# Memory attention phases: the value projection with memory tokens stationary, and the first query weights ahead of the constants

## The reference, cut to what matters

```python
def memory_attention(q_mem, mem_n, w_mem_kv):      # mem_n: (b, 256, 1024), w_mem_kv: (1024, 2048)
    q = q_mem.reshape(b, t, 4, 256) * (256 ** -0.5)
    kv = (mem_n @ w_mem_kv).reshape(b, m, 2, 4, 256)
    k, v = kv[:, :, 0], kv[:, :, 1]
    s = einsum('bthd,bmhd->bhtm', q, k)
    return einsum('bhtm,bmhd->bthd', softmax(s), v)
# in both layers: h = rmsnorm(x, pre_g[i]); mem_n = rmsnorm(mem, mem_g[i]); proj = h @ w_in -> ..., q_mem, gate z
# x = x + rmsnorm(concat(mixer * gate, memory * gate) @ w_out[i], post_g[i])
```

## Time and profile before

| | |
|---|---|
| median of 3 executions | 2368.26 us |
| the profiled execution: its time | 2366.96 us |
| the profiled execution: its span, first to last instruction | 2365.2 us |
| PE busy | 2187.3 us (92%) |
| PE weight loads (beside the matmuls) | 1876.9 us (79%) |
| DVE busy | 1080.8 us (46%) |
| POOL busy | 913.2 us (39%) |
| ACT busy | 729.9 us (31%) |
| granted clock, mean | 0.969 |
| layer 0's V units | about 79 to 134 us of the span |
| layer 1's V units | about 1175 to 1238 us |

### The profile page before, as it was taken

How to read it: one execution, slowest core, us unless ns; L and a number is a source line. 1 busy time by engine, 2 the same in 40 slices (tenths; PEclk the granted TensorE clock), 3 DMA queues, 4 the chain that set the end, 5 groups by cost and what they waited for, 6 DMA issues and landing times. The chain is left out here.

```text
span 2365.2 us, 32257 instructions
## 1 busy us (share of the span) xinstructions
PE 2187.3 (92%) x13362; PEld 1876.9 (79%) x13362; DVE 1080.8 (46%) x1686; ACT 729.9 (31%) x1662; POOL 913.2 (39%) x624
## 2 busy tenths in 40 slices
PE   6989999899999999985989999799999999999995
PEld 5778887688788888874768887688888888888884
DVE  3203333686787778774650223123432334333235
ACT  3113122343343335342322221032423233242332
POOL 3533332232333332331643332444544444454443
PEclk9999999899999999997999999899999999999998
DMA  5221112334222322222631110232222212212111
GB/s 173 78 63 48 54 54 75 107 80 131 81 90 63 116 72 90 63 71 81 195 118 51 54 48 33 61 124 62 62 70 61 59 56 62 70 58 66 54 45 54
DMA packets 228622, 180.59 MB, mean 76 GB/s; under 512 B 23323, under 2 KB 204859, under 8 KB 228475
## 3 DMA queue, kind: packets, MB, share of 16 engines
q1 hardware_dynamic: 228475, 178.52, 24.4%
HBM read 168.71 MB, written 12.21 MB: 76 GB/s over the span
## 5 line engine op out<-in xcount | busy, mean ns | idle before, releaser
L214 PE MATMUL bank<-Hh,Wh 128*128 128x256 f32 (+1 forms) x2192 | 756.4, 345 | 31.5 <-POOL Wl L191 13.0
L188 POOL TENSOR_SCALAR Wh<-Wraw 128x1024 fp32r<-128x1024 f32 x217 | 243.3, 1121 | 1327.3 <-issue 764.4
L214 PE MATMUL bank<-Hl,Wh 128*128 128x256 f32 (+1 forms) x2192 | 742.1, 339 | 0.0
L214 PE MATMUL bank<-Hh,Wl 128*128 128x256 f32 (+1 forms) x2192 | 740.6, 338 | 0.0
L191 POOL TENSOR_TENSOR Wl<-Wraw,Wh 128x1024 fp32r<-128x1024 f32 x217 | 539.8, 2487 | 18.1
L214 PEld LDWEIGHTS bank<-Hh,Wh 128*128 128x128 f32 x2192 | 420.5, 192 | 81.5 <-issue 24.1
L214 PEld LDWEIGHTS bank<-Hh,Wl 128*128 128x128 f32 x2192 | 419.7, 191 | 44.1
L214 PEld LDWEIGHTS bank<-Hl,Wh 128*128 128x128 f32 x2192 | 420.7, 192 | 40.9 <-issue 1.7
L264 PE MATMUL bank<-Wh,Mh 128*128 128x512 f32 x552 | 224.7, 407 | 47.2 <-issue 20.6
L288 DVE TENSOR_TENSOR acc<-bank,acc 128x512 f32<-128x512 f32 x240 | 165.7, 691 | 220.9 <-PE bank L264 220.1
L264 PE MATMUL bank<-Wh,Ml 128*128 128x512 f32 x552 | 221.5, 401 | 0.0
(11 more groups left out here) (203 smaller groups left out, 2689.7 us busy)
## 6 DMA issues: line engine op xcount, KB each, us to landing
Wraw<-in_na_w_in_dram SPq DMA_DIRECT2D x80, 512.0 KB, 3.7
Wraw<-in_ssd_w_in_dram SPq DMA_DIRECT2D x57, 512.0 KB, 4.0
Wraw<-in_w_out_dram SPq DMA_DIRECT2D x48, 512.0 KB, 3.6
R<-acs_dram SPq DMA_DIRECT2D x16, 1536.0 KB, 6.3
Wraw<-in_w_mem_kv_dram SPq DMA_DIRECT2D x32, 512.0 KB, 3.9
R<-gs_dram SPq DMA_DIRECT2D x32, 128.0 KB, 3.5
macc_dram<-acc SPq DMA_DIRECT2D x1, 3072.0 KB, 10.2
R<-macc_dram SPq DMA_DIRECT2D x6, 512.0 KB, 5.4
```

The source lines that it names most:

```text
L188: pool.tensor_scalar(Wh[:, s, :], Wraw[:, s, :], 1.0, 1.0, ALU.mult, ALU.mult).then_inc(pool_c, 1)
L214: mm = pe.matmul(DB[h.k % 2][:, 0:t1 - t0], w[:, k, :], x[:, k, t0:t1], start=(k == 0 and i == 0), stop=(k == KC - 1 and i == 2))
```

## The change

V units now have the orientation of `pe_out`. Unit 8+u holds 256 rows (two blocks of the contraction) by 512 columns of V; the four token tiles of `Mem_h`/`Mem_l` are stationary, and the 512 weight columns move. Four units make one half of the features, which accumulates in four banks at once: `A[4]`, `A[5]`, `DB[0]`, `DB[1]`. ACT evicts each bank straight into `vtok`. The transposes, `vF` and DVE's copies are gone. The second half takes the banks in the order 2, 3, 0, 1. PE waits for all eight evictions (`v_taken`) ahead of the first query unit. In layer 0 SP now loads both q0 units ahead of the constants.

```diff
-            order = ["kv"] * 16 + ["q0"] * 2
+            order = ["k"] * 8 + ["v"] * 8 + ["q0"] * 2
...
+            V_BANK = [A[4], A[5], DB[0], DB[1]]
+            V_ORDER = [(0, 1, 2, 3), (2, 3, 0, 1)]
...
-                    load_f(sp, wkv, slice(u * P, (u + 1) * P))
+                    if u < 8:
+                        load_f(sp, wkv, slice(u * P, (u + 1) * P))
+                    else:
+                        half, j = (u - 8) // 4, u % 4
+                        load_unit(sp, wkv[j * 256:(j + 1) * 256, D + half * 512:D + (half + 1) * 512]
+                                  .rearrange("(k p) c -> p k c", p=P), 2)
...
+                load_head(0, q_col)
                 if pre is not None:
                     sp.wait_ge(x_norm.turned, 2 * NT)
                     pre.sync(sp, None)
-                load_head(0, q_col)
...
-                def take_v(u):
-                    if u >= 2:
-                        act.wait_ge(v_turned, u - 1)
-                    act_take(act, [lambda b: act.activation(vF[u % 2], b[:, :], ACT.Copy)])
+                def take_v(half):
+
+                    for _ in range(4):
+                        U["act"].next()
+                    for i, t in enumerate(V_ORDER[half]):
+                        if i < 3:
+                            act.wait_ge(v_done, 3 * half + i + 1)
+                        else:
+                            act.wait_ge(unit_done, U["act"].value + 2)
+                        act.activation(vtok[:, t, half * 512:(half + 1) * 512], V_BANK[t][:, :], ACT.Copy)\
+                            .then_inc(v_taken, 1)
...
+                    x_norm.act_turned(act, 0)
                     take_v(0)
-                    for u in range(1, 8):
-                        take_v(u)
-                        if u >= 2:
-                            x_norm.act_turned(act, u - 2)
+                    for i in range(1, NT - 1):
+                        x_norm.act_turned(act, i)
+                    take_v(1)
+                    x_norm.act_turned(act, NT - 1)
...
-                def take_v(u):
-                    dve.wait_ge(v_turned, u + 1)
-                    dve.tensor_copy(vtok[:, :, u * P:(u + 1) * P],
-                                    A[4 + u % 2][:, :].rearrange("p (t f) -> p t f", t=4)).then_inc(v_taken, 1)
...
+                pe.wait_ge(out_added, OF["pe"].value + 2)
+                pe.wait_ge(dense_free, HF["pe"].value + 1)
                 for u in range(8):
-                    pe_dense(pe, kv, H=(Mem_h, Mem_l))
-
-                    pe.wait_ge(dense_free, HF["pe"].value + 2)
-                    if u >= 2:
-                        pe.wait_ge(v_taken, u - 1)
+                    half, j = u // 4, u % 4
+                    w, s = U["pe"], U["pe"].k % 2
+                    pe.wait_ge(w_ready, w.value + 3)
+                    wh = Wh[:, s, :].rearrange("p (k c) -> p k c", k=2)
+                    wl = Wl[:, s, :].rearrange("p (k c) -> p k c", k=2)
+                    for i, t in enumerate(V_ORDER[half]):
+                        tok = slice(t * P, (t + 1) * P)
+                        if u == 0 and i == 3:
+                            pe.wait_ge(dense_free, HF["pe"].value + 2)
+                        if half and j == 0:
+                            pe.wait_ge(v_taken, V_ORDER[0].index(t) + 1)
+                        for k in range(2):
+                            for p, (x, y) in enumerate(((Mem_h, wh), (Mem_l, wh), (Mem_h, wl))):
+                                mm = pe.matmul(V_BANK[t][:, :], x[:, 2 * j + k, tok], y[:, k, :],
+                                               start=(j == 0 and k == 0 and p == 0), stop=(j == 3 and k == 1 and p == 2))
+                        if i == 3:
+                            mm.then_inc(unit_done, 1)
+                        elif j == 3:
+                            mm.then_inc(v_done, 1)
+                    w.next()
                     if u >= TURN_X - 8 >= 0:
                         x_norm.pe(pe, u - TURN_X + 8)
-                    for t in range(4):
-                        mm = pe.transpose(A[4 + u % 2][:, t * P:(t + 1) * P], vF[u % 2][:, t * P:(t + 1) * P],
-                                          ident[:, :])
-                    mm.then_inc(v_turned, 1)
+                pe.wait_ge(v_taken, 8)
                 x_norm.pe_end(pe)
```

More of the change, by code:

```diff
@@ L479, in memory_phase @@
                 post_gain = r(D)
-                vF = [post_gain[:, 0:512], post_gain[:, 512:1024]]
                 macc, res = mem[:, 0:2, :], mem[:, 2:4, :]
                 post = [r(NT) for _ in range(3)]
-            else:
-                vF = [mem[:, 2, 0:512], mem[:, 3, 0:512]]
             with ExitStack() as kv_only:
@@ L494, in memory_phase @@
             gain_landed = sem(n + "gain_landed")
-            v_turned, v_taken, scored, max_ready, prob_ready, prob_normed = (
-                sem(n + x) for x in ("v_turned", "v_taken", "scored", "max_ready", "prob_ready", "prob_normed"))
+            v_done, v_taken, scored, max_ready, prob_ready, prob_normed = (
+                sem(n + x) for x in ("v_done", "v_taken", "scored", "max_ready", "prob_ready", "prob_normed"))
             p_turned, pT_ready, mixed, gate_ready, hi_ready = (
@@ L534, in halves @@
             def halves(units):
-                return sum(1 if u == "kv" else 0 if u[:3] == "out" else 2 for u in units)
+                return sum(1 if u == "k" else 0 if u == "v" or u[:3] == "out" else 2 for u in units)
+            V_BANK = [A[4], A[5], DB[0], DB[1]]
+            V_ORDER = [(0, 1, 2, 3), (2, 3, 0, 1)]
             def evicted(name):
@@ L648, in scalar @@
                         x_norm.act_turned(act, u - TURN_X)
-                    for u in range(8):
-                        take_v(u)
+                    for half in range(2):
+                        take_v(half)
                 else:
@@ L877, in tensor @@
                     pe.wait_ge(pT_ready, h * 3 + 3)
-                    pe.wait_ge(v_taken, 8)
                     v = vtok[:, :, h * 256:(h + 1) * 256]
```

## The result

| | before | after |
|---|---|---|
| median | 2368.39 us (4 executions, 2364.78 to 2369.49) | **2345.75 us** (4 executions, 2343.75 to 2350.09) |
| ratio, 95% interval | 1 | **0.9909** [0.9892, 0.9927] |
| the profiled execution: time, span | 2366.96, 2365.2 us | 2344.77, 2343.1 us |

Forecast 2345.1 us, in a range of 2339 to 2351: 22.6 us were gained by the medians, 21.8 were forecast. The steps held less exactly than the sum: the changed parts gave 2.2 us less than I wrote, and chance gave it back in the profiled execution. (The profiled execution of experiment 11 took 4732 us for a cause that its trace does not show; it is left out of all numbers.)

The account below looks back on a forecast made before the run. PE, busy 92% of the span, was taken as the bound. Gains of 10.1 us in layer 0 and 11.7 in layer 1 sum to 21.8, so 2366.96 becomes 2345.1 us, range 2339 to 2351.

Parts of the forecast that it names:

- The seams: PE's idle and transposes between old V units, 1.27 us each; the seven waits inside layer 0's phase should have no successor.
- the end: When PE could start the next matmul after a unit's last: 0.23 us behind that last matmul's start.
- The price of a V matmul: V units: 0.2266 us a matmul as in the output projection, so 24 matmuls cost 5.44 us.
- my upper bound of 5.54: V unit's time at the old shape's matmul price: 5.54 us, 1.5 us more over 15 units.
- The queue: Layer 0 loads: z0's weights 28.33 us behind unit 17's load; the wait moves from q0 to z0, lasting 7.4 us.
- The slow start at z0: Layer 0 behind the wait at z0: clock 0.50 costs 1.98 us as before; could be 2 less or up to 2 more.
- Layer 1's tail: From the last V unit's end to q0 in layer 1: 4.0 us instead of 5.1, gain 1.1.
- The sum: Whole program: 10.1 us from layer 0 plus 11.7 from layer 1, 21.8 us gained.
- (a): Rival at layer 0's z0: the wait vanishes because the constants pass quicker, 2335.7 us; chance 8%.
- (b): Rival in the V phase: POOL's splits or slow loads bound it, a unit taking 5.8 us, 2350.5 us; chance 5%.
- (c): Rival in the V phase: bank turns leave PE idle and the clock drops to 0.50, 2432 us; chance 4%.
- (d): Rival in layer 0: something other than the constants held q0's weights, q0 at 136.85, 2351 us; chance 5%.

Follow-up runs that it names:

- experiment 11: The changed kernel run again unedited, beside the kernel before: ratio 0.9918, four executions of 2345.2 to 2352.1 us.
- experiment 8: Changed kernel, but layer 1's V matmuls take stationary tiles from Mh and Ml instead of Mem_h and Mem_l: 2345.84 us, one execution.
- experiment 10: Changed kernel plus whole-row ssd_d, two later PE waits, and layer 1's memory tokens aligned to 64 bytes at byte 129216: 2341.53 us, ratio 0.9881.
- experiment 12: Changed kernel plus whole-row ssd_d, two later PE waits, and both layers' memory tokens at a multiple of 128 bytes: 2332.11 us, ratio 0.9841.
- experiment 3: Changed kernel with ssd_d loaded as whole rows of 32 numbers, DVE picking the halves out: 2338.24 us, ratio 0.9869.
- experiment 5: Changed kernel with one of ssd_d's two single-number transfers kept, the other half taken from a whole row: 2337.68 us, ratio 0.9868.
- experiment 1: Changed kernel with SP's old order, the constants again between the loads of units 15 and 16: 2353.53 us, ratio 0.9935.
- experiment 4: Changed kernel with the two ssd_d transfers, still 4-byte runs, issued from ACT's queue early in the V phase: 2352.72 us, ratio 0.9929.

## Why the prediction was right, and where it was not

- **The seams.** All seven of layer 0's idle stretches are gone, and no wait for `v_taken` came at unit 12. q0 starts 0.85 behind the end and at 123.52, forecast 123.6. But this agreement is two errors: V began 1.19 us earlier by chance, and seven units took 1.12 us more than forecast.
- **The price of a V matmul** is the step that failed: "24 matmuls cost 5.44 us", taken from the earlier trace rows as having "the same moving tile and shape". It measured 5.60 and 5.62, above my upper bound of 5.54 too, and in layer 1 above the 5.6 that I had named as a sign of being wrong. The rows priced the shape rightly and left out where the stationary operand lies: `Mh` at a multiple of 128 bytes, `Mem_h` 64 or 96 above one (experiments 8, 10, 12). It cost 0.8 us at z0 (five units, since that wait hangs on unit 13's end) and 1.3 in layer 1 (7 x 0.18), less 0.3 for five tiles at 0.88 us, forecast 0.94.
- **The queue.** The step "28.33 us from the load ahead to the first weights behind" held to 0.1 us in three orders. The wait moved from q0 to z0 and lasts 6.76 us, forecast 7.4: unit 17's load left at 115.44 in place of 115.83 (1.19 early with all the rest, 0.8 late by its five units), and z0's weights came 0.5 earlier with it, while q0 began as forecast.
- **The slow start at z0** was taken as 1.98 us, as before. From z0's start to the split behind its first unit it took 158.49 - 147.21 = 11.28 us, where before, without a wait, it took 8.69 (159.82 to the split below), so 2.6 us: 0.6 more, within its bound.

Timeline of POOL in the kernel before, the split behind z0's first unit:

```profile
168.51 1.05 POOL L188 TENSOR_SCALAR Wh<-Wraw 128x1024 fp32r<-128x1024 f32 x1 [4.82 <-issue]
```

- **Layer 1's tail.** ACT begins the last high part at 1217.63, 0.69 behind the end (0.80 forecast), DVE at 1218.76, q0 starts 4.0 behind the end, as forecast.
- **The sum.** 8.8 + 10.75 = 19.6 us, where the text has 21.8. The profiled execution came to 2344.77 only with 1.19 us at its start and 2.3 at its end that are no part of the change. Right to 0.03% was luck; right to 0.1% would have been earned. How much luck, experiment 11 says: four more executions of the same kernel have a median of 2351.1.
- **The rivals.** (a) fell: the passage is constant, even when other loads surround it, and experiments 3 and 5 name what it is made of. (b) fell by its mechanism, though a V unit did get longer: POOL waits 2.07 us for PE at each unit. (c) fell: clock 1.00 from 79 to 122. The rule on depth-cycling of the Trainium skill (TensorE: Matmul & The Clock Gate, "A second HAM failure mode: psum-queue depth-cycling") was not put to the test: it tells of small idle gaps, and with four open banks PE had none, 43.00 us busy of 43. (d) fell by experiment 1 against the change: 4.7 us at the same place, and a wait of 13.44 us at q0.

## What to carry to other kernels

When a matmul's price is read from another place of the program, compare where both operands lie in a partition as well as their shapes, and put the operands of long matmuls at a multiple of 128 bytes; here that was 3% of a matmul. A transfer made of single numbers stopped SP's loads here, whether SP or ACT issued it: load whole rows and let an idle engine pick the numbers out. A reordering that fills a wait is worth what the wait is then, so price it together with what shortens the work in front of it.

## What the runs showed of the hardware that I had not expected

- Two transfers of 1024 numbers of 4 bytes hold the DMA for 16 to 18 us at a share of 0.05 and 0 GB/s, and loads of 512 KB on another engine's queue stand still too (experiment 4).
- The distance between matmuls of 512 columns depends on where the tokens' tensor begins: 0.2267 to 0.2277 us at a multiple of 128 bytes, 0.2333 at 64 above one, 0.2343 at 96, as stationary operand (experiments 8 and 12, the change). As moving operand it is 0.2271 to 0.2277 at a multiple, 0.2290 or 0.2333 at 64 and 0.2334 at 96.
- The same idle stretch of PE (3.60 us) is followed by the low clock in some executions and by the full one in others; which of them it is moves the span by 2.4 us (45.5 against 43.1 us from the last split to the end).
